# Two gate blocks moved behind the first output projection, the second tile's merge moved behind the first gathers, query weights loaded in three parts

## The reference, cut to what matters

```python
xn = rms_norm(h, norm1_g)
parts = xn @ w_in                       # q, k, v, ... and gate_nsa, gate_mla (1024 columns each)
y_nsa = o_nsa @ w_branch_nsa            # o_nsa, o_mla: attention results, 256 x 512 each
y_mla = o_mla @ w_branch_mla
merged = sigmoid(gate_nsa) * y_nsa + sigmoid(gate_mla) * y_mla
h = h + merged @ w_out
# experts, on x = rms_norm(h, norm2_g)
q = (x @ w_query).reshape(T, 8 heads, 2, 128)
s1, s2 = q[..., 0, :] @ sub_keys_1.T, q[..., 1, :] @ sub_keys_2.T
# top 16 of each, top 16 of their 256 sums -> 16 expert numbers e and softmax weights g per token and head
hdn = gelu(sum_d expert_down[e, d] * x[d])
h = h + sum_{heads, 16} g * hdn * expert_up[e]
out = rms_norm(h, norm_f_g)
```

## Time and profile before

| | before |
|---|---|
| median of 3 runs | 992.37 us (991.61 to 995.02) |
| the profiled execution | 996.04 us, span 994.3 us |
| PE busy | 788.2 us (79%) |
| DVE busy | 540.5 us (54%) |
| POOL busy | 526.7 us (53%) |
| ACT busy | 163.4 us (16%) |
| gathered | 269.00 MB of 308.52 MB moved |
| DMA engines' busy share from 246 us on | 0.96 to 0.99, save for the last 50 us |

### The profile page before, as it was taken

The page is one execution under the profiler, slowest core; times in us unless marked ns, Lnnn a source line. Parts: engine busy times, 40 slices in busy tenths (PEclk is TensorE's granted clock), DMA queues, the critical chain, the costliest instruction groups (busy, mean ns, idle before and its releaser), DMA issues.

```text
span 994.3 us, 8041 instructions
## 1 busy us (share of the span) xinstructions
PE 788.2 (79%) x2390; PEld 393.9 (40%) x2390; DVE 540.5 (54%) x1451; ACT 163.4 (16%) x508; POOL 526.7 (53%) x632
## 2 busy tenths in 40 slices
PE   6999999998759887748874977597668948777685
PEld 3886455545335333224422433243234324222231
DVE  2222454325969665565656566565556666655434
ACT  1220332212022020202111111102020202011011
POOL 7600000002667666676665666566756666667664
PEclk9999999999979999988997999799978988998999
DMA  9933280162999999998999999999989999999996
GB/s 262 240 120 148 87 337 1 67 272 65 376 383 354 357 371 363 362 400 325 368 358 369 357 356 370 344 378 372 362 319 372 362 401 347 359 375 379 352 371 246
DMA packets 107178, 308.52 MB, mean 310 GB/s; under 512 B 28672, under 2 KB 31488, under 8 KB 106112
## 3 DMA queue, kind: packets, MB, share of 16 engines
q0 software_dynamic: 73904, 269.00, 71.7%
q1 hardware_dynamic: 28096, 38.87, 11.7%
q10 hardware_dynamic: 5136, 0.15, 0.4%
HBM read 306.40 MB, written 1.05 MB: 309 GB/s over the span
## 4 chain that ended last, share of the span: by engine, by line
PE 40%; POOL 16%; another core or an unknown queue 14%; DMA 13%; issue 11%; DVE 4%; ACT 1%; SPq 0%; POOLq 0%; DVEq 0%; ACTq 0%
PE bank L1141 35%; POOL region_w L508 16%; DMA region_w<-in_expert_up,chosen 7%; DMA region_w<-in_expert_down,chosen 4%; PE xn_ps L1141 3%; PE bank L1146 2%; DVE region_w L1048 1%; DMA region_q<-in_w_in 1%; PE bank L1317 0%; ACT pool_bd L704 0%; DVE region_q L929 0%; ACT pool_bd L567 0%; PE xn_ps L1146 0%; DVE x_sb L1070 0%
## 5 line engine op out<-in xcount | busy, mean ns | idle before, releaser
L1141 PE MATMUL bank<-region_w,pool_bd 128*128 128x512 f32 x994 | 481.7, 625 | 100.5 <-DMA region_w<-in_expert_up,chosen 60.7
L1048 DVE CUSTOM_DVE_ANT_0 region_w<-xn_ps,region_w 128x1024 f32<-128x1024 f32 x256 | 312.0, 1221 | 216.0 <-DMA region_w<-in_expert_down,chosen 182.3
L508 POOL DMA_INDIRECT region_w<-in_expert_up,chosen x256 | 244.9, 956 | 166.5 <-issue 66.4
L1141 PEld LDWEIGHTS bank<-region_w,pool_bd 128*128 128x128 f32 x994 | 186.0, 198 | 368.6 <-issue 356.3
L508 POOL DMA_INDIRECT region_w<-in_expert_down,chosen x256 | 243.3, 951 | 102.9 <-issue 76.7
L704 ACT ACTIVATE pool_bd<-ident,pool_bd 128x128 f32<-128x128 f32 x250 | 84.3, 392 | 196.0 <-PE bank L1141 130.0
L500 POOL TENSOR_TENSOR stat<-stat 128x1 f32<-128x1 f32 x2 | 0.4, 199 | 176.1 <-ACT gates L666 176.1
L1141 PE MATMUL bank<-region_q,xT 128*128 128x512 f32 (+3 forms) x224 | 86.9, 522 | 1.3 <-DMA region_q<-in_w_in 1.3
L1146 PE MATMUL bank<-ident,pool_bd 128*128 128x128 f32 x32 | 8.7, 362 | 82.6 <-ACT pool_bd L567 62.0
L567 ACT ACTIVATE pool_bd<-bank 128x256 f32<-128x256 f32 (+2 forms) x47 | 18.0, 385 | 326.0 <-remote 253.0
L1141 PE MATMUL bank<-region_q,oT 128*128 128x256 f32 x256 | 59.2, 380 | 3.5 <-issue 2.8
(11 more groups left out here) (196 smaller groups left out, 549.8 us busy)
## 6 DMA issues: line engine op xcount, KB each, us to landing
region_q<-in_w_in SPq DMA_DIRECT2D x5, 2048.0 KB, 8.2
region_q<-in_w_query SPq DMA_DIRECT2D x1, 8192.0 KB, 22.3
region_w<-in_w_out SPq DMA_DIRECT2D x1, 4096.0 KB, 23.2
region_w<-in_expert_down,chosen POOLq DMA_INDIRECT x256
region_w<-in_expert_up,chosen POOLq DMA_INDIRECT x256
region_q<-in_w_in SPq DMA_DIRECT2D x16, 128.0 KB, 3.1
region_w<-in_wb_nsa SPq DMA_DIRECT2D x1, 2048.0 KB, 13.6
region_w<-in_wb_mla SPq DMA_DIRECT2D x1, 2048.0 KB, 12.7
```

The costliest lines, as they stand in the source:

```text
L508: pool.indirect_dma_start(out=row, out_offset=None, in_=table, in_offset=bass.IndirectOffsetOnAxis(ap=chosen[s % PICKS][:, k:k + 1], axis= ...
L1048: dve.tensor_tensor_reduce(out=row, in0=xn_ps[:, :], in1=row, scale=1.0, scalar=0.0, op0=ALU.mult, op1=ALU.add, accum_out=hdn[:, k:k + 1]) ...
L1141: return pe.matmul(out_, lhsT, rhs, start=start, stop=stop)
```

## The change

- **Gate blocks.** The order of the 8 gate blocks becomes `GATES`. The attention loop does only six of them (48 matmuls, `GATE_EARLY`) instead of eight; those of tile 1, chunks 2 and 3, go behind `w_out(0)`, in small pieces between the steps of the head: 4 matmuls before `normedT(0)`, then one at a time between `query`, `queryT` and `key_scores` of steps 0 and 1, and 7 after `key_scores(1)`.
- **Sigmoid.** The pass `0.5 * tanh + 0.5` over the gates (DVE, two instructions) goes; `gated` does (tanh + 1) * y, and the copy behind `mergedT` scales by 0.5.
- **Tile 1's merge.** `branch(1, 0)` no longer stands before `normedT(0)`; all four `branch(1, n)` follow the last gate matmul. `query(2)` comes before `mergedT(1)` and `w_out(1)`. On DVE `gated(1, n)` and `merge(1, n)` move from behind `choose(0)` into the loop of dots, after dot 9 of step 0; in their old place stand 7 turns of `choose(1)`.
- **Memory.** The down ring moves to `region_q` (four buffers where attention's data lay, four on chunk 6), the up ring to the place of the branch weights. `w_query` comes in three transfers: heads 0 and 1 when the attention results are copied (`ot_cp` 4), heads 2 and 3 into chunk 7's half when the last gate matmul is done (`a_mm` 22), heads 4 to 7 into the place of `w_out` when `w_out(1)` is done (`wo_mm` 4).
- **POOL's order.** 8 downs, then one up and two downs at a time, instead of 16 downs and then up and down in turn. The first up waits for `branch(1, 1)` (`y_mm` 6) instead of for `w_out(1)`.

```diff
-CHUNK_UNITS = (2, 7, 10, 14, 16, 18, 20, 22)
+CHUNK_UNITS = (2, 7, 10, 14, 16, 18, 21, 22)
-        wq = view(region_q, 0, KC, 2048)
+        wq01 = view(region_q, 8192, KC, 512)
+        wq23 = view(region_q, 4096, KC, 512)
-        ring_dn = view(region_w, 0, RING, 1024)
-        ring_up = view(region_w, 8192, RING, 1024)
+        wq47 = view(region_w, 8192, KC, 1024)
+        ring_dn = [view(region_q, 12288 + 1024 * r, 1024) for r in range(4)] + [view(region_q, 1024 * r, 1024) for r in range(4)]
+        ring_up = view(region_w, 0, RING, 1024)
+        GATES = ((0, 0), (0, 1), (1, 0), (1, 1), (2, 0), (3, 0), (2, 1), (3, 1))
+        GATE_EARLY = 6 * KC
+
         def gate_upto(n):
-            return min(GATE_MM, GATE_PRE + (GATE_MM - GATE_PRE) * (n + 1) // (len(UNITS) + 1))
+            return min(GATE_EARLY, GATE_PRE + (GATE_EARLY - GATE_PRE) * (n + 1) // (len(UNITS) + 1))
+
+        def gate_bank(v):
+            return 6 + v % 2 if v < 6 else v - 6
...
             sp.dma_start(wbm, a["wb_mla"].rearrange("(k p) n -> p k n", p=P)).then_inc(wbm_in, 16)
+            load_chunk(6)
             sp.dma_start(wo, a["w_out"].rearrange("(k p) n -> p k n", p=P)).then_inc(wo_in, 16)
+            load_chunk(7)
...
             sp.wait_ge(ot_cp, 4)
+            sp.dma_start(wq01, query_columns(0, 2)).then_inc(wq01_in, 16)
             sp.wait_ge(a_mm, CHUNK_UNITS[-1])
-            sp.dma_start(wq, a["w_query"].rearrange("(k p) n -> p k n", p=P)).then_inc(wq_in, 16)
+            sp.dma_start(wq23, query_columns(2, 2)).then_inc(wq23_in, 16)
             sp.wait_ge(wo_mm, 4)
             sp.dma_start(gfb, a["norm_f_g"].rearrange("(o n) -> o n", o=1).broadcast_to([P, DM])).then_inc(gf_in, 16)
+            sp.dma_start(wq47, query_columns(4, 4)).then_inc(wq47_in, 16)
...
-            pool.wait_ge(y_mm, 6)
-            for n in range(SLOTS):
+            pool.wait_ge(ot_cp, 4)
+            for n in range(RING):
+                if n == RING // 2:
+                    pool.wait_ge(a_mm, CHUNK_UNITS[-2])
+                down(n)
+            done = RING
+            for n in range(HEAD):
+                if n == 0:
+                    pool.wait_ge(y_mm, 6)
                 if n == RING // 2:
                     pool.wait_ge(y_mm, 8)
-                down(n)
-            pool.wait_ge(wo_mm, 4)
-            for n in range(LAG):
                 up(n)
-                down(SLOTS + n)
-            for n in range(LAG, 2 * LAG):
-                up(n)
-                down(SLOTS + 2 * n - LAG)
-                down(SLOTS + 2 * n - LAG + 1)
-            for n in range(2 * LAG, STEPS * SLOTS):
+                down(done)
+                down(done + 1)
+                done += 2
+            for n in range(HEAD, STEPS * SLOTS):
...
             query_copy(1)
             queryT_copy(1)
-            mergedT_copy(1)
+            gate_tanh(act, 6)
+            softmax_exp(0)
+            gate_tanh(act, 7)
             softmax_exp(1)
             query_copy(2)
             queryT_copy(2)
+            mergedT_copy(1)
...
-            dve.wait_ge(a_cp, 22)
-            for t in range(2):
-                link(dve.tensor_scalar(out=gt[:, t, :], in0=gt[:, t, :], scalar1=0.5, scalar2=0.5, op0=ALU.mult, op1=ALU.add))
...
-            for n in range(1, 4):
-                gated(1, n)
-            for half in range(2):
-                merge(1, half)
-            picking = None
+            picking = choose(1)
+            for _ in range(EARLY_TURNS):
+                next(picking)
...
+                    if s == 0 and k == 9:
+                        for n in range(4):
+                            gated(1, n)
+                        for half in range(2):
+                            merge(1, half)
```

More of the change, by code:

```diff
@@ L356, in up_row @@
             low, slot, _ = up_place(n)
-            return (ring_dn if low else ring_up)[:, slot, at]
+            return ring_dn[slot][:, at] if low else ring_up[:, slot, at]
         def up_landed(n):
@@ L647, in _ @@
                     done += 1
-            while done < 8:
+            while done < 6:
                 gate_tanh(act, done)
@@ L971, in _ @@
             norm2(0)
-            gated(1, 0)
             def top16(*searches):
@@ L1087, in _ @@
                     dve.wait_ge(xn_in, 2 * tile_of(s) + 2)
[L1088 to L1089 removed]
+                if s == 1:
+                    picking = choose(2)
                 for k in range(SLOTS):
@@ L1470, in _ @@
             w_out(0)
-            branch(1, 0)
+            gate_step(GATE_EARLY + 4)
             normedT(0)
+            gate_step(GATE_EARLY + 5)
             pe.wait_ge(xt2_cp, 2)
-            pe.wait_ge(wq_in, 16)
             query(0)
+            gate_step(GATE_EARLY + 6)
             queryT(0)
+            gate_step(GATE_EARLY + 7)
             key_scores(0)
+            query(1)
+            gate_step(GATE_EARLY + 8)
+            queryT(1)
+            gate_step(GATE_EARLY + 9)
+            key_scores(1)
+            gate_step(GATE_MM)
             pe.wait_ge(h_ready, 2)
-            for n in range(1, 4):
+            for n in range(4):
+                if n < 2:
+                    pe.wait_ge(a_cp, 21 + n)
                 branch(1, n)
-            query(1)
-            queryT(1)
-            mergedT(1)
-            key_scores(1)
-            pe.wait_ge(y_used, 8)
-            w_out(1)
             query(2)
@@ L1489, in _ @@
             key_scores(2)
+            mergedT(1)
+            pe.wait_ge(y_used, 8)
+            w_out(1)
             pe.wait_ge(mg_cp, 4)
```

47 lines of the change are left out of this document (26 added, 21 removed).

## The result

The kernel before took 993.18 us in the runs made beside the changed one (median of 4, 991.61 to 995.02), the changed kernel 1005.03 us (median of 4, 1004.32 to 1007.19). The ratio is 1.0125, 95% interval 1.0102 to 1.0147: 12 us slower, where 1.6 were forecast, and above the range's 1001. The profiled execution after took 1005.36 us with a span of 1003.6, against 996.04 and 994.3 before, so the span grew by 9.3.

What follows compares the result with a forecast made beforehand. PE was taken to bound the front up to the first gather, and a DMA stream of 269 MB the rest. Terms -10.7 + 0.95 + 11.3 = +1.6 us on 992.37 gave 994.0 us, range 985 to 1001.

Steps and rivals of the forecast that it cites:

- Step 1: Attention loop: 16 gate matmuls leave it, gaining 10.7 us, with bounds of 7 and 13.8.
- Step 2: Head: three single gate matmuls cost 0.95 us, the others nothing; first gather near 231.1.
- Step 3: Gather stream: 6.3 MB of query weights enter it, `w_out(1)` ends at +45.3 without a DMA gap; 11.3 us lost.
- The term of 11.3 us: Gather stream: put 4.1 MB behind by the weight loads, made up at 364 GB/s; bounds 15.3 us and nothing.
- Step 4: Start of the dots: earlier `choose(1)` and other rings give 0, bounds 3 us gained or 3 lost.
- Rival B: `query(4)` waits 7 us for its load and stops the weighing: 3 to 7 us more, 999 us; chance 0.20.
- Rival A: Gather stream takes the weight bytes into unused DMA rate: 988.3 us if half, 982.7 if all; chance 0.30.
- C: DVE bounds the shortened attention loop, so the gain is only 7 us: 997.7 us; chance 0.14.
- D: The gathers don't start earlier, as one waits for `ot_cp` or `a_mm`; no chance worth counting.

Runs made afterwards that it cites:

- paced pair: Changed kernel and kernel before, each with one POOL memset behind each gather, on a prompt chip: 925.80 against 923.08 us.
- small_again: Changed kernel, but all gathers except the first 8 down and 8 up fetch 1024-byte rows, on a late chip: 1001.68 us, ratio 1.0069.
- merge5: `wout_first` with the second tile's gated and merge passes behind dot 5 instead of dot 9 of step 0: 1008.85 us, ratio 1.0092.
- two_heads: Changed kernel with heads 2 to 7 computed from the columns of heads 0 and 1, so 6.3 MB of `w_query` are not loaded: 1009.35 us, ratio 1.0107.
- wout_first: Changed kernel with `mergedT(1)` and `w_out(1)` ahead of `queryT(2)`, and ACT copying `mergedT(1)` before query 2: 1009.85 us, ratio 1.0107.
- after_again: Changed kernel, unaltered, run again on a late chip: 1008.43 us, ratio 1.0135.
- pause_again: Changed kernel with merge behind dot 5, `mergedT(1)` before `query(2)`, and POOL's 18th gather waiting for `mergedT(1)`'s copies, on a late chip: 990.42 us, ratio 0.9976.
- gates_loop: Changed kernel with all eight gate blocks back inside the attention loop, none in the head: 1020.03 us, ratio 1.0199.
- pause_gates_loop: The kernel of `pause_again` with all eight gate blocks back in the attention loop, on a late chip: 1005.56 us, ratio 1.0090.

## Why the prediction was wrong, by its own steps

- **Step 1, the loop: right.** `branch(0, 0)` begins at 178.12 instead of 188.53, 10.4 us earlier where 10.7 were forecast, with waits of PE as foreseen. One of them, in the kernel after, in a unit with one gate matmul:

```profile
168.13 0.70 PE L1164 MATMUL bank<-pool_bd 64*128 64x256 f32 x4 [0.37 <-DVE mxs L954]
```

- **Step 2, the head: right.** First gather at 230.82, forecast 231.1.
- **Step 3, the bytes: the failing step**, in two places. The sub-steps hold for the branches, which end at +15.9 (+16.5), and for the merge, at +30.0 (+28.7). Query 2 ends at +27.2 instead of +21.5, for it waits 5.66 us for its 2.1 MB, a wait that the sum did not have. Then "`w_out(1)` ... +45.3" and "no gap". It ended at +64 (294.87 less 230.82), since I let PE's signals reach ACT at no cost ("transposes and copies 2.6") and gave no thought to what such a signal takes under the gathers. That was not a new effect of the change. It stood in the trace of before in most queries from query 3 on (13.4 us at query 9), and I had not looked at what ACT waits for there. There it holds PE at queries only: the copies of `mergedT(1)` were made at 246.33, 5.5 us behind the first gather, and came at once. POOL did not wait for `w_out(1)` either: its first up gather, at 264.56, follows the last down with a gap of 0.30 us. The change put `mergedT(1)` and `w_out(1)` behind query 2's round trip and behind 27 us of gathers. POOL then waits 25 us, and the DMA engines' queue covers 10 of them: 15 us of nothing. From the first gather to the last (240.85 to 981.28 before, 230.82 to 990.88 after) the stream grows by 19.6 us, past the 15 at which I said that I would be wrong, and -10.0 + 19.6 is the 9.3 of the spans but for 0.3. On the prompt chip, in the paced pair, it grew by 13.5, inside my bounds of 8 and 15: the step failed by the late round trip, and the rest of it holds about as told.
- **The term of 11.3 us** was mis-sized for a late chip. It rested on the stream being bound by the DMA engines at a share of 0.96. `small_again` moves little over a third of the bytes at a share of 0.32 and is 0.6% quicker than the changed kernel. With the hole gone the 6.3 MB measure 6.3 us, with 1.8 to 10.8 left open. The two mistakes are of opposite sign; by the measured terms the sum is -10.0 + 6 + 15 = +11, against +12 measured, and with 4.5 us open in one term the fit is no proof.
- **Step 4: about nothing, not tested alone.** `merge5` moves the merge and changes nothing, with its transposes behind `query(2)` all the same.
- **Rival B happened and didn't count.** Step 0 of the weighing after:

```profile
316.80 5.87 PE L1164 MATMUL bank<-region_w,oT 128*128 128x256 f32 x16 [7.34 <-DMA region_w<-in_w_query]
```

PE waits the 7 us that I gave it, and POOL 4.45 us at up slot 14. But `two_heads`, without that wait, is no faster than `wout_first` with it. The transfer was issued at 295.45 and used 21.4 us later, against 20.5 by an even share, but the share was not quite even: from 296 to 316 the plain loads moved 4.72 MB and the gathers 3.04. The load of 2.1 MB, issued at 233.0, was used 19.4 us later, where an even share gives 10.2: from 240 to 248 it moved 1.13 MB in 557 packets beside 2.06 MB in 567 packets of the gathers. By the rule of the Trainium skill ("DMA: Bandwidth & Descriptors", section "Queues, rings and completion order") an engine takes turns between its queues, a packet at a time. The trace agrees in the second case, by the packets as the profile counts them and not by the bytes: with half the bytes in each packet a load gets a third of the rate. I had taken the 2.1 MB at the full rate, 5.1 us.
- **Rival A** described the right symptom (bytes that are nearly free) for the wrong reason. **C** and **D** did not happen.

Shown: the hole; the late signal in front of `w_out(1)` that makes it; that the weight loads don't make the signal late; that the place of the merge, `mergedT(1)` ahead of `query(2)` and a stop of POOL together take 1.6% back (`after_again` against `pause_again`, one chip), and that with all gate blocks in the loop 1.1% come back though POOL never stops (`gates_loop` against `pause_gates_loop`); that the lateness doesn't need the bytes. Not shown: what makes a signal late. It was seen only while gathers were in flight, but `pause_gates_loop` has both a prompt and a late one under unbroken issuing and full DMA engines. In the kernel before none is late until the first up gather (264.56); a stream of downs alone was not run. Nor is it shown why it differs between chips, and by which way (PE standing before `queryT`, or late `up_used` signals) it costs the long stream 70 us.

## What to carry to other kernels

Before moving work under a stream of gathers, look at what the round trips between engines already take there: compare the end of the producer's row with the start of the consumer's, and take a long "remote" as a price, not as noise. A chain of several such signals belongs in front of the stream. Where it can't be, put the long work that the buffers wait for (`w_out(1)` here) in front of the next round trip and not behind it, so that a late signal runs beside it. A DMA share near 1 doesn't prove that bytes are the bound: fetch a quarter of each row and see whether the time falls. And when a run is meant to slow an engine, read the spacing from its trace before reading its time: the memset here went into a gap.

## What the runs showed of the hardware that was not expected

- Under gathers issued back to back from POOL, a signal from PE to ACT came up to 26 us after the end of the matmuls (17 to 20 us in most runs of the late chips, query 2 of `two_heads` 26), at a DMA share of 1.03 and at 0.32 alike. It was prompt when POOL had just stopped (`pause_again`, a share of 1.03) and also once when it had not (`pause_gates_loop`, 1.02). With two up gathers fewer in flight it was 2 to 11 us.
- A memset of 0.14 us behind each gather on POOL left them 1.25 us apart instead of 1.24: it fits into the 0.30 us between two gathers.
- A plain load beside the gathers shared the DMA engines packet for packet (557 to 567 in 8 us), so that one with packets of 2 KB moved 1.13 of 3.20 MB.
- The same kernel takes 922 us on one kind of chip and 994 to 999 on the other, and one with a third of the bytes 895 and 1002. On the former the gathers of whole rows run at 409 GB/s. In the profiled executions TensorE's mean granted clock was 0.985 to 0.993 there and 0.917 to 0.951 on late chips, where PE stands more.
